# Decays moved between latent attention steps, branch norms one by one, and a mixing product that keeps six sums open

## What is computed

```python
proj = h @ w_in
y_a = sc_b * depthwise_conv(sc_c * sc_h, w_sc_conv)
la_f = log_sigmoid(ga_f @ w_gla_a_up[0] + b_gla_a[0]) / GLA_TAU
o = gla_scan(q, k, v, la_f, True) + flip(gla_scan(flip(q), flip(k), flip(v), flip(la_b), False))
y_b = rms_norm(o, g_gla_head) * silu(gg)
y_c = blocked_attention(q_c, k_c, v_c, ...)
y_d = silu(layer_norm(depthwise_conv(a * sigmoid(gate), w_cfm_dw), g_cfm_ln, b_cfm_ln))
y = concatenate([rms_norm(yb, gb) for yb, gb in zip((y_a, y_b, y_c, y_d), gains)])
h = layer_norm(DN_ALPHA * h + y @ w_out, ln1_g, ln1_b)
h = layer_norm(DN_ALPHA * h + conv_ffn(h, w_ffn_up, w_ffn_dw, w_ffn_down), ln2_g, ln2_b)
```

## Time and profile before

| | us |
|---|---|
| median of 3 executions | 3748.5 (3744.82 to 3751.92) |
| the profiled execution: time | 3759.01 |
| the profiled execution: span | 3757.2 |
| PE busy in it | 3503.3 (93%) |
| DVE busy | 2414.3 (64%) |
| ACT busy | 1722.1 (46%) |
| mean granted clock of PE, as a share of full speed | 0.938 |

### The profile page before, as it was taken

How to read it: one execution, slowest core, us unless ns; L and a number is a source line. 1 busy time by engine, 2 the same in 40 slices (tenths; PEclk the granted TensorE clock), 3 DMA queues, 4 the chain that set the end, 5 groups by cost and what they waited for, 6 DMA issues and landing times.

```text
span 3757.2 us, 43728 instructions
## 1 busy us (share of the span) xinstructions
PE 3503.3 (93%) x13658; PEld 2457.4 (65%) x13658; DVE 2414.3 (64%) x2918; ACT 1722.1 (46%) x2332; POOL 486.0 (13%) x624
## 2 busy tenths in 40 slices
PE   7988799998988799998998988979999999999996
PEld 3447468885438458886564555458778877778884
DVE  3453465653454346555455776059999999999995
ACT  2234142322225233323221113048888878788884
POOL 0000000000000000000000000023434343444341
PEclk9985899999995799999999999989999999999998
DMA  4121122232112123332112001349999999999995
GB/s 175 62 62 62 61 74 94 93 94 73 62 45 79 56 67 96 96 94 94 54 47 77 6 23 60 97 157 355 368 353 370 362 366 351 361 355 370 361 366 190
DMA packets 167697, 618.84 MB, mean 165 GB/s; under 512 B 18497, under 2 KB 18625, under 8 KB 166881
## 3 DMA queue, kind: packets, MB, share of 16 engines
q1 hardware_dynamic: 156768, 573.84, 42.7%
q0 software_dynamic: 10816, 43.52, 4.1%
HBM read 587.92 MB, written 29.36 MB: 164 GB/s over the span
## 4 chain that ended last, share of the span: by engine, by line
PE 58%; DVE 15%; issue 14%; POOL 5%; ACT 4%; DMA 3%; POOLq 1%; DVEq 0%; SPq 0%; ACTq 0%
PE bank L576 53%; DVE w_part L2394 5%; PE bank L1087 4%; DVE sb_rstd L1688 2%; DMA sb_ring<-in_w 2%; POOL pick L542 1%; POOL sb_work L488 1%; DVE sb_work L2427 1%; POOL y_rows L548 1%; DVE sb_work L2422 1%; DVE sb_work L2191 0%; DVE sb_turn_tables L2187 0%; DVE sb_work L2424 0%; DVE sb_work L2215 0%; ACT sb_work L1291 0%
## 5 line engine op out<-in xcount | busy, mean ns | idle before, releaser
L2394 DVE TENSOR_TENSOR w_part<-sb_ring,w_part 128x1024 fp32r<-128x1024 f32 x762 | 889.1, 1223 | 70.2 <-ACT w_part L1593 44.7
L1593 ACT ACTIVATE w_part<-sb_ring 128x1024 fp32r<-128x1024 f32 x762 | 768.5, 1053 | 85.9 <-PE bank L1087 48.4
L1087 PE MATMUL bank<-w_part,xg_hi 128*128 128x512 f32 x2048 | 564.0, 397 | 0.0
L576 PE MATMUL bank<-h_hi,split_part 128*128 128x512 f32 x1408 | 444.0, 400 | 8.3 <-ACT h_hi L1361 8.3
L1087 PEld LDWEIGHTS bank<-w_part,xg_hi 128*128 128x128 f32 x2048 | 383.1, 188 | 89.2
L576 PE MATMUL bank<-sb_work,sb_ring 128*128 128x512 f32 (+5 forms) x880 | 331.9, 532 | 10.5 <-DVE sb_modv L1678 10.5
L1087 PE MATMUL bank<-w_part,xg_lo 128*128 128x512 f32 x1024 | 321.2, 395 | 0.0
L576 PEld LDWEIGHTS bank<-h_hi,split_part 128*128 128x128 f32 x1408 | 267.8, 190 | 74.9 <-issue 8.4
L1087 PE MATMUL bank<-w_part,act_hi 128*128 128x512 f32 x1024 | 284.9, 400 | 2.0 <-DVE act_lo L2437 0.6
L576 PE MATMUL bank<-sb_hT,sb_ring 128*128 128x512 f32 (+1 forms) x608 | 272.0, 605 | 11.4 <-ACT sb_hT L1178 11.4
L576 PE MATMUL bank<-sb_work 128*128 128x64 f32 (+6 forms) x992 | 233.4, 441 | 45.5 <-DVE sb_work L1916 22.8
(11 more groups left out here) (344 smaller groups left out, 4905.7 us busy)
## 6 DMA issues: line engine op xcount, KB each, us to landing
sb_ring<-in_w SPq DMA_DIRECT2D x768, 512.0 KB, 6.9
sb_ring<-in_wstream SPq DMA_DIRECT2D x304, 512.0 KB, 3.5
y_rows<-sb_padc POOLq DMA_DIRECT2D x1, 4096.0 KB, 27.3
sb_xT<-in_x SPq DMA_DIRECT2D x1, 2048.0 KB, 11.5
x_rows<-sb_padc SPq DMA_DIRECT2D x1, 2048.0 KB, 22.7
residual<-sb_hT POOLq DMA_DIRECT2D x1, 2048.0 KB, 6.6
sb_hT<-residual POOLq DMA_DIRECT2D x1, 2048.0 KB, 8.2
x_rows<-sb_work SPq DMA_DIRECT2D x1, 2048.0 KB, 6.6
```

The lines of the kernel that those rows point to most:

```text
L576: ins = nc.tensor.matmul(out, l, r, start=start, stop=stop)
L1087: ins = nc.tensor.matmul(out[n][:], l[:, k, :], r[:, n * 512:(n + 1) * 512], start=False, stop=(k, p) == (KD - 1, 2))
L1593: nc.scalar.activation(w_hi[t % SPLITS], ring[:, t % RING, :], ACT.Copy).then_inc(s_hi, 1)
L2394: nc.vector.tensor_tensor(w_lo[t % SPLITS], ring[:, t % RING, :], w_hi[t % SPLITS].bitcast(F32), ALU.subtract).then_inc(s_lo, 1)
```

## The change

- **Decays.** `decay(piece)` puts the chain of stage 3 between the attention steps, one piece per step, on DVE from step 1 on, between the taps and the reciprocal; DVE now does the taps ahead of the reciprocal. ACT has its share in steps 2 (Exp and Ln) and 9 (Exp). The clears go to POOL, `kdec` in two halves.
- **Projections.** Beside the attention steps PE runs 7 projections, in steps 0 to 12. The values of the gated attention and the projections gg0 and gg1 go behind the attention and behind the four blocks of stage 4.
- **Norms.** The squares of cfm and of branches 0 and 2 are taken on DVE in blocks 1 and 2, their sums on PE and roots on ACT in block 3, into `deviations`; branches 3 and 1 follow.
- **Mixing.** `mix_part` adds two input tiles at a time; six output tiles have their PSUM banks and ring slots open at once and take branch 0, then 2, then 3, then 1.
- **Modulation.** Two tiles stay behind block 1, two each at ln1 and ln2; 18 per layer go behind tiles 2, 5, ..., 53 of the feed-forward network.

```diff
-BESIDE_AT = {0: "k", 1: "gv0", 2: "gv2", 3: "c0", 4: "h0", 5: "c1", 6: "h1", 7: "b0", 8: "b1", 14: "gg0", 15: "gg1"}
-MOD_STEP = 10
+BESIDE_AT = {0: "c0", 2: "h0", 4: "c1", 6: "h1", 8: "b0", 10: "b1", 12: "k"}
+PADS_STEP = 8
+DECAY_STEP = 1
...
+                pool.wait_ge(dve_done, when("query", l, HEADS - 1))
+                nc.gpsimd.memset(qdiag, 0.0).then_inc(pool_done, did.up(("qdiag_zero", l)))
+                pool.wait_ge(act_done, when("exps", l, HEADS * TB - 1))
+                nc.gpsimd.memset(kdec[:, 0], 0.0).then_inc(pool_done, did.up(("kdec_zero", l, 0)))
+                pool.wait_ge(pe_done, when("full", "turn", l, HEADS * TB - 1))
+                nc.gpsimd.memset(kdec[:, 1], 0.0).then_inc(pool_done, did.up(("kdec_zero", l, 1)))
...
+                token_values(l, 0)
+                pe.wait_ge(dve_done, when("norm_in", ("cfm", l)))
+                chunks(("mean", ("cfm", l)), lambda k: ones_mix, lambda k: proj[:, k, :], 2)
+
+                def variance(tag, rows_of):
+
+                    chunks(("var", tag), lambda k: ones_mix, lambda k: rows_of[:, k, :], 2, ready=("square", tag))
+
                 for j in range(TB):
-                    modulation(("gla", l, j))
                     for d in range(2):
                         pe.wait_ge(dve_done, when("kdec", l, j, d))
                         out = bank("gdiag", l, j, d)
                         for i in range(NSUB):
                             mm(out[:, i * 64:(i + 1) * 64], kdec[:, d, i, :], qdiag[:, d, j, i * 64:(i + 1) * 64],
                                True, True, *(("gdiag", l, j, d) if i == NSUB - 1 else ()))
+                    if j == TB - 1:
+                        variance(("cfm", l), early_squares["cfm"])
+                        for b in (0, 2):
+                            variance(("branch", l, b), early_squares[b])
...
+                    if j == 0:
+                        token_values(l, 2)
+                    if j == 1:
+                        modulation(("gla", l))
+                    if j >= 2:
+                        project(l, ("gg0", "gg1")[j - 2])
                 pe.wait_ge(dve_done, when("amat", l))
                 for h in range(HEADS):
                     values(("yb", l, h), vtok, lambda s: amat(h)[:, s, :], h)
-                for c in range(2):
-                    norm(("gla", l, c), sq, c, 1, const("heads64"), center=False)
-
-                modulation(("cfm", l))
-                norm(("cfm", l), proj, 0, 2, ones_mix)
-                for b in range(4):
-                    norm(("branch", l, b), sq, 2 * b, 2, ones_mix, center=False)
-                for b in range(4):
+                    if h >= 2:
+                        norm(("gla", l, h - 2), sq, h - 2, 1, const("heads64"), center=False)
+
+                def mix_part(w, out, m, ks):
+
+                    for k in ks:
+                        mm(out[:], w[:, k, :], yn[:, k, :], k == 0, k == 3, *(("mix", l, m) if k == 3 else ()))
+
+                opened = [(tile().rearrange("p (k m) -> p k m", m=P), bank("mix", l, m)) for m in range(MIX_OPEN)]
+                for b in (0, 2, 3):
                     pe.wait_ge(dve_done, when("normed", ("branch", l, b), 1))
+                    for m, (w, out) in enumerate(opened):
+                        mix_part(w, out, m, (2 * b, 2 * b + 1))
+                    if b == 0:
+                        variance(("branch", l, 3), early_squares[3])
+                    if b == 2:
+                        variance(("branch", l, 1), sq[:, 2:4, :])
+                pe.wait_ge(dve_done, when("normed", ("branch", l, 1), 1))
                 for m in range(KD):
-                    w = tile().rearrange("p (k m) -> p k m", m=P)
-                    chunks(("mix", l, m), lambda k: w[:, k, :], lambda k: yn[:, k, :], KD)
+                    if m < MIX_OPEN:
+                        mix_part(*opened[m], m, (2, 3))
+                    else:
+                        w = tile().rearrange("p (k m) -> p k m", m=P)
+                        mix_part(w, bank("mix", l, m), m, (0, 1, 4, 5, 6, 7, 2, 3))
...
+                    if t in MOD_BEHIND:
+                        modulation(("ff", l, t))
...
+                    if i == DECAY_STEP + 1:
+                        for d in range(2):
+                            act.wait_ge(dve_done, when("la_abs", l, d))
+                            nc.scalar.activation(e_la[:, d, :], e_la[:, d, :], ACT.Exp, scale=-1.0).then_inc(act_done,
+                                did.up())
+                        for d in range(2):
+                            act.wait_ge(act_done, did.all_but(1))
+                            nc.scalar.activation(e_la[:, d, :], e_la[:, d, :], ACT.Ln, bias=const("ones")[:,
+                                0:1]).then_inc(act_done, did.up(("la_log", l, d)))
+                    if i == DECAY_STEP + 8:
+                        for d in range(2):
+                            act.wait_ge(dve_done, when("qdiag_arg", l, d))
+                            nc.scalar.activation(z_la[:, d, :], z_la[:, d, :], ACT.Exp).then_inc(act_done,
+                                did.up(("qdiag_exp", l, d)))
...
+                    if j < 2:
+                        keep_values(2 * j)
+                    if j == TB - 1:
+                        for i, tag in enumerate((("cfm", l), ("branch", l, 0), ("branch", l, 2))):
+                            deviation(tag, out=deviations[:, i, :])
...
+                    if j == TB - 2:
+                        keep("gg0")
                 did.note("amat_off", l)
+                nc.scalar.activation(proj[:, SLOT["gg0"], :], proj[:, SLOT["gg0"], :], ACT.Silu).then_inc(act_done,
+                    did.up(("gate_gg0", l)))
+                keep("gg1", ACT.Silu)
...
+                    if i == PADS_STEP:
                         for c in range(2):
                             dve.wait_ge(act_done, when("proj", l, f"c{c}"))
                             dve.wait_ge(act_done, when("proj", l, f"h{c}"))
                             dve.wait_ge(dve_done, did.n)
                             nc.vector.tensor_tensor(pads[:, c, 1:T + 1], proj[:, SLOT["c0"] + c, :],
                                 proj[:, SLOT["h0"] + c, :], ALU.mult).then_inc(dve_done, did.up())
-                    if MOD_STEP + 1 < i < MOD_STEP + 5:
+                    if PADS_STEP < i < PADS_STEP + 4:
                         dve.wait_ge(dve_done, did.n)
-                        short_taps(i - MOD_STEP - 2)
+                        short_taps(i - PADS_STEP - 1)
+                    decay(i - DECAY_STEP)
+                    dve.wait_ge(act_done, when("exps", l, i))
...
+                scaled(("cfm", l), proj, proj, 2, lambda k: col(l, "cfm_g", k), deviations[:, 0, :])
+                dve.wait_ge(act_done, when("norm_out", ("cfm", l), 1))
+                branch(0, deviations[:, 1, :])
...
+                branch(2, deviations[:, 2, :])
+                branch(3)
+                branch(1)
...
+MOD_BEHIND = tuple(range(2, 56, 3))
+MIX_OPEN = 6
...
-        spots += [(("kv", l), 1)]
-        spots += [(("gla", l, j), n) for j, n in enumerate((10, 1, 1, 1))]
-        spots += [(("yb", l), 2), (("cfm", l), 2), (("var", ("branch", l, 3)), 4)]
-        spots += [(("var", (name, l)), 1) for name in ("ln1", "ln2")]
+        spots += [(("gla", l), 2)]
+        spots += [(("var", ("ln1", l)), 2)] + [(("ff", l, t), 1) for t in MOD_BEHIND] + [(("var", ("ln2", l)), 2)]
```

261 lines of the change are left out of this document (126 added, 135 removed).

## The result

| | before | after |
|---|---|---|
| median of 4 executions each, one chip | 3748.58 us (3744.82 to 3751.92) | 3656.78 us (3653.01 to 3660.84) |
| ratio, 95% interval | | 0.9752 (0.974 to 0.9765) |
| profiled execution, span | 3759.01, 3757.2 us | 3656.11, 3654.3 us |
| PE busy; DVE; ACT | in the table of before | 94%; 66%; 47% |
| mean granted clock | 0.938 | 0.963 |

The account below looks back on a forecast made before the run. Poorly used mixer stretches (decays, gated-attention blocks, values and norms) and a PE-bound feed-forward network were taken as the limits; per layer -39.3 + 6 - 52.6 + 6 + 33.1 = -46.8, two layers -93.6, giving 3655 us, range 3624 to 3689.

Parts of the forecast that it names:

- Attention, -39.3 forecast: From the scores to the first `gdiag`: decays beside the attention and four projections gone start the first block at 258.8, not 298.1.
- One of the prediction's own signs of being wrong: In the attention stage: the prediction is wrong if DVE idles over 30 us there.
- DVE becomes the engine that sets the step: 69.5 + 13.7 = 83.2 us: In the attention: with four projections gone, DVE's old work plus the decay chain limits each step, 83.2 us before waits.
- the rule's 1.38 us more: ACT's table loads in the attention: the Trainium skill adds a drain per switch, by which the sum would be 5.5 us later.
- Clears, 0 forecast: Clears moved from DVE to POOL beside the attention: taken as costing 0, with 2 us carried as uncertainty.
- The rival that a clear holds the scalings up: In the attention: DVE's scalings wait for POOL's large clear, 23.8 us per layer, 3703 us; chance 0.14, shared with longer head waits.
- Blocks, +6 forecast: Four gated-attention blocks: fuller clock saves, the wait for gg0 (+4.7) and six sums (+5.3) cost; +6 us, ends +1 and +14.
- Values and norms, -52.6 forecast: From values product to mixing: early norms and open sums leave 13 us of 65.6; ends -56 and -44.
- Mixing, +6 forecast: Mixing product: two more pairs of sums (3.5 us) and branch 2's norm some 2.4 us late; ends +3 and +10.
- Modulation in the feed-forward network, +33.1 forecast: Feed-forward network: 18 modulation tiles of 1.84 us at full clock, uncovered, lengthen each layer; ends 33 and 41.
- The slower rival: Feed-forward network: each of 36 modulation bursts loses 3.8 us to lower clock, 137 us in all, 3792 us; chance 0.04.
- The rival with full clock in the attention and blocks: Clock stays full in attention, blocks and mixing product: 14 us less per layer, 3627 us; chance 0.12.

Follow-up runs that it names:

- the run with eight: GpSimd clears the large buffer eight times over instead of once, against the changed kernel: 3675.26 us, +18 us.

## Why the prediction was right

**Attention, -39.3 forecast, -38.5 measured.** The end at 250 and the first `gdiag` near 259 came as forecast, but by a working that was partly wrong, so the closeness of this term is in part luck. One of the prediction's own signs of being wrong came true: DVE idles over 30 us in the attention, 35.1 us in the stage. From DVE's first maximum to its last scaling I had 103 us: 83.2 of work, 2 of gaps, 3 of wait in step 3 and 15 behind the heads. The trace has 107.0 (135.97 to 242.94): 79.5 of work, 3.2 of gaps, 2.6 in step 3 and 21.7 in the other waits for ACT, behind the heads and behind the projection that follows each. The work was put too high, the waits too low, and the 4 us added for the half clock, with a sum of 248.8 taken as 250, made up for it.

The step that failed behind a right number is "DVE becomes the engine that sets the step: 69.5 + 13.7 = 83.2 us". The run with the decays behind shows that they lengthen the attention by only 7.2 us, about half of their own length: a step is set by a chain over all three engines (maximum, exponential, scaling, turn), and DVE's other work lies partly in its waits. Most of the 39 us comes with the PE work that left the stage, the four projections, though no run shows their share alone; the decays' own move is 3 us a layer. What shortened the gap from 31.3 to 19.1 us is known in part: the ten tiles were 4.6 us of it (the run with their move alone, 26.7); the clears that left DVE, the values now made there and the order account for the other 7.6 together, and no run takes them apart.

**Table switches.** 1.28 us each by the row; the row held and the rule's 1.38 us more did not show.

**Clears, 0 forecast, 0 measured.** The price is 3.51 and 0.95 us, near the lower bound; the upper bound of 23.8 us came from an unlike operation (TENSOR_SCALAR to fp32r) and was 7 times too high. The rival that a clear holds the scalings up is a true mechanism (the run with eight), and it did not act because of where the clear stands. The reason that I gave against it, that DVE's waits would absorb it, was not the one that counted.

**Blocks, +6 forecast, +6.0 measured.** The wait behind gg0 was put at 4.7 us and is 5.16; the six sums at 5.3 and are 6.95. What the step missed is that the two are one: the wait costs the clock as well, and without it the stage is 9.9 us shorter in layer 0, and 9.4 in layer 1, where 5 us a layer were expected.

**Values and norms, -52.6 forecast, -50.1 measured.** 13 us were forecast and 15.5 came. PE's own work alone is 13.0; the wait for the root of head norm 0, which the term named, is 1.09 us, and one of 1.44 us for ACT's square of the second pair of heads it did not hold.

**Mixing, +6 forecast, +4.5 measured.** The two pairs of sums take 3.5 us as forecast. The wait for branch 2 was put at 2.4 us and is 0.70.

**Modulation in the feed-forward network, +33.1 forecast, +33.3 measured for the whole stretch.** Single tiles leave the clock full. The slower rival (bursts that cost the clock) needed 2.6 us for each of 36 bursts to undo the gain. Twelve bursts of three cost 4.0 us each and eighteen of two 2.2: a real price, 48 and 39 us in all, which is about half of the gain. The rival was refuted only for bursts of one. The reason against it, dense work on both sides, does not carry: in the runs with longer bursts the same dense work stands on both sides.

The rival with full clock in the attention and blocks (-14 us a layer) did not come: the clock is 0.88 and 0.78 there.

The forecast's range of 3624 to 3689 held. The terms are off by +0.8, +2.5, -1.5 and +0.2 us a layer, in sum +2.0.

## What to carry to other kernels

Work that is used as filler under a wait costs little there (7.4 us a layer for 19 tiles) and its full length elsewhere: take the wait away first, then move the filler, and try the parts alone to see which needs which (here +42 us alone, inside -92 together). Keep bursts of light matmuls between heavy ones as short as the program allows, and read not only the burst but the rows behind it. A wait of PE can cost its length and then the clock of what follows: here the end of one wait of 5 us, in a stage at clock 0.78, gave 8 to 10 us a layer. A forecast can land on its number with two wrong terms: check the idle time of the engine that it calls the limit.
